# An earlier start of the output projection, an eleventh chunk place and gates that travel with the row numbers, in a two-layer RWKV-7 / latent-attention encoder with experts

## The chip, the cores and the metric

The kernel runs on one core of a Trainium2 chip. The metric is the device time in microseconds (us) of one execution, as the median of several runs; lower is better. Engines are named as in the profile: PE (TensorE), PEld (its weight loads), DVE (VectorE), ACT (ScalarE), POOL (GpSimd), SP (SyncE, which here only issues DMAs).

## The reference

One sequence of 512 tokens, width 1024, two layers. Layer 0 mixes tokens by a bidirectional RWKV-7 recurrence (16 heads of 64), layer 1 by multi-head latent attention. Behind either mixer stands an expert-choice mixture of experts: each of 16 experts takes the 64 tokens that score highest for it.

```python
for i in range(DEPTH):                        # DEPTH = 2
    h = rms_norm(x, norm_mix_g[i])
    if i % 2 == 0:
        mix = rwkv7_time_mix(h, ...)          # ends in (y * g) @ w_o
    else:
        mix = mla_mix(h, ...)
    x = x + mix
    x = x + expert_choice_ffn(rms_norm(x, norm_ffn_g[i]), ...)

def expert_choice_ffn(h, w_router, w_gate, w_up, w_down):
    aff = softmax((h @ w_router).astype(float32), axis=-1)
    gates, idx = top_k(swapaxes(aff, 1, 2), 64)          # per expert
    xe = h[b_idx, idx]
    hid = silu(xe @ w_gate) * (xe @ w_up)                # 1024 x 1024 each
    ye = (hid @ w_down) * gates[..., None]
    return zeros_like(h).at[b_idx, idx].add(ye)
```

The expert weights are 2 layers x 16 experts x 3 matrices of 4 MB, all float32; each is read once.

## The kernel before

**The recurrence (layer 0)** runs over eight pairs of heads (`pairs_pe`, `pairs_act`, `pairs_dve`, `pairs_pool`, u = 0 to 7). In each pair PE first multiplies keys and queries (`across`, L833), then inverts small triangular blocks in five levels (`inverse_step`, L875: X, then T and U, with DVE and ACT copies between), then forms state matrices (L1005 to L1057) and runs a chain of seven state steps (L1088, L1070, L1077). While it waits it computes projections of the next pair, one matmul of 128x512 at a time (`proj_piece`, L547). The last pair has no next one: there nothing stands in those gaps. The end of a pair (centre, square, variance, root on POOL, scale, transpose, times gate) is `last_y_...` for the last pair; `ydone_ready` counts finished pairs.

**The output projection** (`out_pe`, L1388) takes eight tiles `out(t, z)`: four blocks of 128 tokens by two halves of 512 columns, each a sum over eight k, one for each pair of heads, so 64 matmuls of 128x512. For layer 0 all of it stands behind the last pair; only what needs the last pair's result waits for it. DVE adds each tile to x (`added`, L1520), and then each block of tokens is squared (ACT), given its root and multiplied by the norm's gain (POOL, L1495 to L1508), transposed (L1398) and multiplied with the router (L1407). `route_dve` makes the softmax, the eight rounds of top-8 (L1574, L1576), the slot numbers, and with `picks` the matrices `pick` (tokens by 2 x 64 slots, ones and zeros) and `pick_gate` (the same times the gates).

**The experts** run over eight pairs of experts (`moe_pe`, i = 0 to 7). A pair uses twelve chunks of weights of 2 MB; `load_chunk` puts chunk g into place g mod 10 (`RING` = 10), and SP issues it when chunk g - 10 has been read by PE (`chunk_read`); chunk 10, the first refill, comes in two halves, the first when half of chunk 0 is used, and chunk 95 in four. The first ten are loaded while PE still projects and routes: chunks 0 to 3 and 8 after `ydone_ready`, then three blocks of normed tokens are stored to memory (`store_tokens`), then 4, 5, 6 and, after the router, 7 and 9. For the first pair of experts PE gathers the tokens by 32 matmuls with `pick` (`gather_first_pe`, L1648), for the others POOL gathers rows from memory by an indirect DMA (L1759) with row numbers that PE and DVE make (`rows_pe` L1637, `rows` L1765). ACT makes tanh into one buffer `th`, DVE makes the two products (L1772, L1777) into `hid`, PE transposes it (L1702), multiplies with the down weights, and adds the experts' rows to the tokens by `combT`, the transposed `pick_gate` (L1658, L1729).

## Time and profile before

| | us |
|---|---|
| median of 3 runs | 2003.29 |
| lowest and highest run | 2002.77, 2010.22 |
| the profiled execution, device time | 2009.6 |
| its span, first to last instruction | 2007.7 |
| mean granted TensorE clock | 0.975 |

The span is what the views below cut up; the profiled execution is 1.9 us longer than its span and 6.3 us longer than the median. In a timeline row the columns are start, duration, engine, line, operation, written<-read and the number of merged instructions; in brackets the idle time of that engine ahead of it and what ended it. A float32 matmul is recorded as two (x16 is eight matmuls of the program). Spans are in us from the first instruction. The last pair of heads lies at 605 to 664 us, the output projection and the routing of layer 0 behind it to 751, its experts to about 1212; routing and experts of layer 1 take 1464 to the end.

### The profile page before, as it was taken

The page shows a single profiled execution, that of the slowest core. Times are in us where ns is not written, and L with a number is a line of the kernel's source. Part 1 is how long each engine was busy: PE and PEld are TensorE (multiplying, and loading weights), DVE is VectorE, ACT ScalarE, POOL GpSimd, SP SyncE. Part 2 cuts the span into 40 slices and gives each one's busy share as a digit, 9 for nine tenths or more (in the row PEclk, how much of TensorE's full clock was granted, in tenths as well). Part 3 has the DMA queues.
Part 4 walks back from the last instruction along what each step waited for, and adds up shares of the span by engine and source line. Part 5 has one row for each costly group of instructions (what it writes and reads, how often), then busy time and mean ns, then how long its engine had stood idle before and what let it go on. Part 6 is the DMA issues. An engine that isn't in the chain of part 4 may idle for free.

```text
span 2007.7 us, 44887 instructions
## 1 busy us (share of the span) xinstructions
PE 1825.1 (91%) x19992; PEld 955.6 (48%) x19992; DVE 798.5 (40%) x1448; ACT 519.6 (26%) x1025; POOL 239.9 (12%) x294
## 2 busy tenths in 40 slices
PE   7899999999997959999988889899995999999987
PEld 4466666666656534333333325566643333333332
DVE  6755755655654241222121113677714211122111
ACT  2344344344443110101101102465511111010100
POOL 2203113213213110000000001112110000000000
PEclk9999999999999979999999999899997999999999
DMA  4101011011003758999999990300064999999997
GB/s 124 35 27 35 24 32 36 24 32 36 24 10 119 273 210 343 426 429 426 428 427 427 427 405 33 117 23 23 12 274 188 410 426 428 427 427 428 426 427 315
DMA packets 85002, 459.98 MB, mean 229 GB/s; under 512 B 16710, under 2 KB 49867, under 8 KB 60235
## 3 DMA queue, kind: packets, MB, share of 16 engines
q1 hardware_dynamic: 82794, 449.78, 54.9%
q0 software_dynamic: 2016, 7.34, 0.9%
q8 instruction: 159, 2.61, 0.5%
q14 instruction: 33, 0.26, 0.0%
HBM read 449.23 MB, written 7.86 MB: 228 GB/s over the span
## 4 chain that ended last, share of the span: by engine, by line
PE 61%; DMA 21%; issue 7%; DVE 5%; ACT 2%; DVEq 1%; POOL 1%; POOLq 1%; SPq 0%; ACTq 0%; PEldq 0%; another core or an unknown queue 0%
DMA arena<-in_moe_w_down 18%; PE banks L1683 17%; PE banks L547 9%; PE banks L875 5%; PE banks L1388 5%; PE banks L1729 5%; DMA arena<-in_moe_w_up 2%; PE banks L2190 2%; PE banks L2055 2%; PE banks L833 1%; PE banks L2215 1%; PE banks L2203 1%; PE banks L1648 1%; PE banks L564 1%; PE banks L824 1%
## 5 line engine op out<-in xcount | busy, mean ns | idle before, releaser
L1683 PE MATMUL banks<-arena 128*64 128x512 f32 x3072 | 684.2, 598 | 53.1 <-DMA arena<-in_moe_w_down 35.9
L1683 PEld LDWEIGHTS banks<-arena 128*64 128x64 f32 x3072 | 222.3, 137 | 478.5 <-issue 434.3
L1788 DVE TENSOR_TENSOR arena<-arena,banks 128x512 f32<-128x512 f32 x128 | 88.0, 688 | 330.2 <-PE banks L1729 330.2
L547 PE MATMUL banks<-arena 128*128 128x512 f32 x384 | 187.2, 613 | 2.6 <-ACT arena L587 2.6
L875 PE MATMUL banks<-arena 64*64 64x64 f32 x7168 | 148.0, 225 | 32.3 <-issue 27.0
L875 PEld LDWEIGHTS banks<-arena 64*64 64x64 f32 x7168 | 135.6, 139 | 76.5 <-issue 62.7
L1227 POOL TENSOR_TENSOR arena<-arena 128x512 f32<-128x512 f32 x80 | 102.6, 1309 | 436.4 <-DVE arena L1284 436.4
L1742 ACT ACTIVATE arena<-banks 128x512 f32<-128x512 f32 x32 | 19.1, 597 | 411.1 <-PE banks L1683 411.1
L1729 PE MATMUL banks<-arena 128*128 128x512 f32 x256 | 113.7, 597 | 3.0 <-ACTq L1751 3.0
L1777 DVE SCALAR_TENSOR_TENSOR arena<-arena,banks 128x512 f32<-128x512 f32 x32 | 33.7, 1052 | 206.6 <-PE banks L1683 206.6
L1309 DVE TENSOR_TENSOR arena<-banks,arena 128x512 f32<-128x512 f32 x80 | 52.5, 687 | 142.7 <-PE banks L875 142.2
L1388 PE MATMUL banks<-arena 128*128 128x512 f32 x242 | 106.6, 595 | 1.8 <-POOLq L400 1.3
L1759 POOL DMA_INDIRECT arena<-out_dram,small x14 | 13.6, 969 | 779.8 <-DVE small L1765 718.7
L547 PEld LDWEIGHTS banks<-arena 128*128 128x128 f32 x384 | 66.6, 189 | 68.6 <-issue 62.0
L1772 DVE SCALAR_TENSOR_TENSOR arena<-arena,banks 128x512 f32<-128x512 f32 x32 | 22.0, 688 | 186.9 <-ACT arena L1742 186.9
L1750 ACT COPY arena<-banks 64x512 f32<-64x512 f32 x64 | 37.1, 580 | 179.0 <-PE banks L1683 178.6
L1729 PEld LDWEIGHTS banks<-arena 128*128 128x128 f32 x256 | 47.3, 190 | 59.4 <-issue 58.2
L1745 ACT COPY arena<-banks 128x512 f32<-128x512 f32 x32 | 18.8, 586 | 206.1 <-PE banks L1702 206.1
L1388 PEld LDWEIGHTS banks<-arena 128*128 128x128 f32 x242 | 44.9, 190 | 55.3 <-issue 55.3
L1165 ACT COPY arena<-banks 128x512 f32<-128x512 f32 x64 | 38.2, 597 | 108.6 <-PE banks L875 108.6
L2055 PE MATMUL banks<-arena 128*128 128x192 f32 (+1 forms) x320 | 61.7, 347 | 1.1 <-DVE arena L1958 1.1
L2190 PE MATMUL banks<-arena 96*128 96x512 f32 x128 | 60.5, 618 | 1.6 <-POOLq L400 1.6
(301 smaller groups left out, 2205.2 us busy)
## 6 DMA issues: line engine op xcount, KB each, us to landing
arena<-in_moe_w_gate SPq DMA_DIRECT2D x64, 2048.0 KB, 36.3
arena<-in_moe_w_up SPq DMA_DIRECT2D x64, 2048.0 KB, 38.2
arena<-in_moe_w_down SPq DMA_DIRECT2D x60, 2048.0 KB, 39.0
out_dram<-arena SPq DMA_DIRECT2D x12, 512.0 KB, 2.7
arena<-in_x SPq DMA_DIRECT2D x8, 512.0 KB, 6.0
arena<-in_rw_wr SPq DMA_DIRECT2D x8, 512.0 KB, 4.9
arena<-in_rw_wk SPq DMA_DIRECT2D x8, 512.0 KB, 3.6
arena<-in_rw_wv SPq DMA_DIRECT2D x8, 512.0 KB, 3.9
```

The source lines that it names most:

```text
L547: last = nc.tensor.matmul(b[:, :], w_sl[:, n, k, :], xmix[n][:, k, :], start=(k == 0), stop=(k == ND - 1))
L875: last = nc.tensor.matmul(v[half[p ^ lands(h, m)], bank, token(n)], st(q, h, m), mv(q, h, m), start=True, stop=True)
L1165: nc.scalar.copy(Tm[:, :, d, :], two_banks(("T", lv, d, u))).then_inc(free[rj[("T", lv, d, u)][0]], 1)
L1227: nc.gpsimd.tensor_tensor(blocks[lv][d].rearrange("p h m j -> p (h m) j"), LRB[d].rearrange("p h m a j -> p (h m) a j")[:, :, 0, :], bc(le ...
L1309: nc.vector.tensor_tensor(Xm[d].rearrange("p (h m) j -> p h m j", h=2), two_banks(name).rearrange("p h (m j) -> p h m j", j=CH), bc(eye.un ...
L1388: last = nc.tensor.matmul(b[:, :], yT[n][:, k, tile(t)], wo_at[n][:, k, z * 512:(z + 1) * 512], start=(k == 0), stop=(k == ND - 1), skip_g ...
L1683: last = nc.tensor.matmul(b[z * CAP:(z + 1) * CAP, :], st[:, k, :], ring[g % RING][:, k, z * 512:(z + 1) * 512], start=(c % 2 == 0 and k = ...
L1729: nc.tensor.matmul(b[:, :], combT[:, t * P:(t + 1) * P], ye[:, z * 512:(z + 1) * 512], start=True, stop=True).then_inc(full[COMB[j]], 1)
L1750: nc.scalar.copy(ye[e * CAP:(e + 1) * CAP, z * 512:(z + 1) * 512], b[z * CAP:(z + 1) * CAP, :])
L1788: nc.vector.tensor_tensor(xs, xs, b[:, :], ALU.add).then_inc(free[COMB[j]], 1)
L2055: last = nc.tensor.matmul(b[:, y * width:(y + 1) * width], cT[:, n0 + j, t * P:(t + 1) * P], w[:, j, :], start=(j == 0), stop=(j == n - 1))
L2190: nc.tensor.matmul(b[:, :], qkT[h][0][0:QK, t * P:(t + 1) * P], qkT[h][1][0:QK, :], start=True, stop=True).then_inc(full[aj[("S", u, h, t) ...
```

## The change

Four things in one edit.

- The DMA scratch is set to 4096 (`dynamic_dma_scratch_size`), the arena grows from 51 to 54 x 1024 floats, `th` and `pick_gate` are gone, and an eleventh chunk place stands in the room: `RING` = 11. Chunk 10 is loaded with the first six.
- Layer 0's output projection starts within the last pair of heads: `part_pe` computes k = 0 to 5 of four of the eight tiles (24 matmuls) between the steps of that pair, three of them are added to x there by DVE (`part_added`), and the fourth (`HELD`) stays in its bank. The weights w_o are loaded one pair earlier, x for three blocks of tokens in the last pair. Behind the pair the order of tiles, squares, transposes and roots is another.
- The gates come through the same small matmul as the row numbers (three columns in place of one, `row_cols`); DVE halves them into `half_gate`, and the second product is multiplied by that in place of 0.5. tanh goes directly into `hid`, and both products work in place there. `combT` is the transposed `pick`.
- In the first pair of experts the gather is in two halves, with the first chunk's matmuls between them.

```diff
-RING = 10
+RING = 11
-        ARENA = 51 * 1024
+        ARENA = 54 * 1024
...
+        EARLY = NPAIR - 2
+        def part_pe(pe, t, z, k):
+            if (t, z, k) == (0, 0, 0):
+                pe.wait_ge(ld_wo[0], 16)
+                pe.wait_ge(ld_y, 16)
+                pe.wait_ge(ydone_ready, EARLY)
+            if k == EARLY:
+                pe.wait_ge(ydone_ready, EARLY + 1)
+            b = open_job(pe, rj, ("part", t, z)) if k == 0 else ps[rj[("part", t, z)][0]]
+            last = nc.tensor.matmul(b[:, :], yT[0][:, k, tile(t)], wo_at[0][:, k, z * 512:(z + 1) * 512], start=(k == 0),
+                                    stop=(k == EARLY - 1 and (t, z) != HELD), skip_group_check=((t, z) == HELD))
...
+                def part_added(t, z):
+                    b = job_full(dve, rj, ("part", t, z))
+                    xs = x_sb[:, t, z * 512:(z + 1) * 512]
+                    nc.vector.tensor_tensor(xs, xs, b[:, :], ALU.add).then_inc(free[rj[("part", t, z)][0]], 1)
                 for lv in range(LEVELS):
+                    if lv == 1 and not more:
+                        dve.wait_ge(ld_x2, 16 * 3)
+                        part_added(0, 0)
...
-                out(0, 0, range(ND - 1))
+                out(2, 0, range(ND - 1))
                 last_y_pe(pe)
-                out(0, 1, range(ND - 1))
+                part_pe(pe, *HELD, EARLY)
+                out(2, 1, range(ND - 1))
+                for t, z in ((0, 0), (0, 1), (1, 1)):
+                    out(t, z, range(EARLY, ND - 1))
                 pe.wait_ge(ydone_ready, NPAIR)
+                for t, z in ((0, 0), (0, 1), (1, 0), (1, 1)):
+                    out(t, z, range(ND - 1, ND))
...
 +            def inverse_root(t):
...
+            for t in range(NT):
+                if layer == 1 or t < NT - 1:
+                    inverse_root(t)
+                if layer == 0 and t == NT - 2:
+                    inverse_root(NT - 1)
...
-            nc.vector.tensor_tensor(by_expert(pick_gate), by_expert(pick), of(aff), ALU.mult).then_inc(gate_picked, 1)
...
                     for h in range(2):
+                        if i == 0 and c == 0:
+                            if h:
+                                gather_half_pe(pe, 1, xj)
+                            else:
+                                rows_pe(pe, 0, layer)
+                                combination_pe(pe, 0, xj)
+                            job_read(pe, xj, ("x", 0, h))
                         chunk_into(name, c + h, xeT[:, 4 * h:4 * h + 4, e * CAP:(e + 1) * CAP])
...
-            for g in (0, 1, 2, 3, KEPT + 1) if layer == 0 else (0, 1, 2, 3, 4, KEPT + 1):
+            for g in (0, 1, 2, 3, KEPT + 1, KEPT + 3) if layer == 0 else (0, 1, 2, 3, 4, KEPT + 1, KEPT + 3):
...
-    nc = bacc.Bacc("TRN2", target_bir_lowering=False, num_devices=1)
+    nc = bacc.Bacc("TRN2", target_bir_lowering=False, num_devices=1, dynamic_dma_scratch_size=4096)
```

Three places show what stands in a row on an engine. The first is PE in the last pair of heads, from the first level of the inversion (L875, after the change L874) to the first state matrices; before the change:

```order
L875 MATMUL banks<-arena 64x64 x224
L897 MATMUL banks<-arena 64x64 x32
L875 MATMUL banks<-arena 64x64 x64
L824 MATMUL banks<-ident,arena 128x128 x4
L875 MATMUL banks<-arena 64x64 x160
L1005 MATMUL banks<-arena 64x128 x32
```

The same place after the change, down to the third level; L911 is `part_pe`:

```order
L874 MATMUL banks<-arena 64x64 x32
L911 MATMUL banks<-arena 128x512 x2
L874 MATMUL banks<-arena 64x64 x64
L911 MATMUL banks<-arena 128x512 x4
L874 MATMUL banks<-arena 64x64 x32
L911 MATMUL banks<-arena 128x512 x3
L874 MATMUL banks<-arena 64x64 x64
L911 MATMUL banks<-arena 128x512 x3
L874 MATMUL banks<-arena 64x64 x32
L896 MATMUL banks<-arena 64x64 x32
```

Twelve wide matmuls have come between the steps of the first two levels; six more follow up to L1042 and six between there and the pair's end.

The second place is PE at the beginning of layer 1's experts (layer 0's reads the same), from the second routing transpose on; before the change:

```order
L1450 MATMUL banks<-ident,arena 128x16 x4
L1648 MATMUL banks<-arena 128x128 x32
L1658 MATMUL banks<-ident,arena 128x128 x4
L1683 MATMUL banks<-arena 64x512 x48
L1702 MATMUL banks<-ident,arena 128x128 x4
```

After it:

```order
L1524 MATMUL banks<-ident,arena 128x16 x4
L1757 MATMUL banks<-arena 128x128 x16
L1744 MATMUL banks<-small,arena 128x3 x4
L1764 MATMUL banks<-ident,arena 128x128 x4
L1789 MATMUL banks<-arena 64x512 x8
L1757 MATMUL banks<-arena 128x128 x16
L1789 MATMUL banks<-arena 64x512 x40
```

Chunk 0 (the first x8 of L1789) now stands behind half of the gather, and chunk 1 behind the other half.

The third place is SP ahead of layer 0's experts; before the change, from the store of pair 5's result on:

```order
L2412 DMA out_dram<-arena 128x512 [waits y_done]
L1368 DMA arena<-in_rw_g 128x128 [waits bank_full6]
L1369 DMA arena<-in_rw_g 32x128
L2420 DMA arena<-in_rw_wo 128x8x1024 [waits bank_full7]
L2422 DMA arena<-out_dram 128x6x512 [waits y_stored]
L1540 DMA arena<-in_x 128x1024 [waits ld_low_rank,ld_projection_v,ld_gate,ld_projection_k,bank_full1,ld_projection_r,bank_full6]
L1540 DMA arena<-in_x 128x1024 x3
```

After it:

```order
L2524 DMA arena<-in_rw_wo 128x8x1024 [waits bank_full6]
L2533 DMA out_dram<-arena 128x512 [waits y_done]
L1421 DMA arena<-in_rw_g 128x128 [waits bank_full6]
L1422 DMA arena<-in_rw_g 32x128
L2542 DMA arena<-out_dram 128x6x512 [waits y_stored,bank_full7]
L1648 DMA arena<-in_x 128x1024 x3
L1648 DMA arena<-in_x 128x1024 [waits ld_low_rank,ld_projection_v,ld_gate,ld_projection_k,bank_full1,ld_projection_r,bank_full6]
```

The output weights have moved ahead of the wait for pair 5, and three of the four blocks of x ahead of the last pair's end.

## Rows read from the trace of the kernel before

**Rows 1.** A stretch: us, busy per engine (instructions), PEclk, DMA share, GB/s
```profile
800.00:900.00 100.00, 100.00 (x452) 37.39 (x450) 22.29 (x32) 10.04 (x18) 1.88 (x2) 1.00 1.01 427
```
**Rows 2.** Waits of PE, 780 to 1200: us in total, times, longest
```profile
PE banks L1683 <- DMA arena<-in_moe_w_down: 18.1, 16, 2.6
PE banks L1683 <- DMA arena<-in_moe_w_up: 7.5, 8, 1.1
PE banks L1683 <- DMA arena<-in_moe_w_gate: 1.4, 2, 1.1
```
**Rows 3.** The chain that ended last: eight out-projection matmuls; last tile added; the router's exp
```profile
687.05 6.87 PE banks L1388 x16
...
724.72 0.69 DVE arena L1520
...
730.73 0.27 ACT arena L1481
```
**Rows 4.** Stretches: pair 6 in three parts, then the last pair
```profile
543.30:566.80 23.50, 23.50 (x419) 13.93 (x418) 7.11 (x11) 10.05 (x17) 10.21 (x8) 1.00 0.01 3
566.80:584.00 17.20, 13.74 (x589) 10.65 (x588) 15.71 (x23) 10.33 (x20) 0.00 (x0) 1.00 0.06 20
584.00:605.30 21.30, 20.38 (x537) 13.52 (x540) 12.57 (x29) 6.29 (x16) 0.00 (x0) 1.00 0.03 7
615.70:630.90 15.20, 9.23 (x413) 8.63 (x413) 5.79 (x9) 5.49 (x11) 9.67 (x8) 1.00 0.35 126
630.90:648.20 17.30, 11.99 (x552) 10.83 (x551) 5.16 (x8) 7.17 (x15) 0.00 (x0) 0.90 0.02 4
648.20:664.10 15.90, 14.08 (x492) 11.41 (x492) 5.93 (x17) 4.33 (x12) 0.00 (x0) 1.00 0.02 5
```
**Rows 5.** PE groups by line, 604 to 664: busy, mean ns, idle before and releasers
```profile
L875 PE MATMUL banks<-arena 64*64 64x64 f32 x896 | 19.5, 229 | 10.9 <-issue 9.7 <-DVE arena L1309 1.1
```
**Rows 6.** Timeline: the last pair's end and the turn of its result
```profile
664.26 6.25 PE L1388 MATMUL banks<-arena 128*128 128x512 f32 x14 [0.54 <-ACT arena L1214]
...
670.93 0.65 PE L824 MATMUL banks<-ident,arena 128*128 128x128 f32 x4 [0.42 <-DVE arena L1259]
```
**Rows 7.** Timeline of SP: chunks 4 and 5, then the last block of tokens
```profile
724.71 0.82 SPq L1797 DMA_DIRECT2D arena<-in_moe_w_gate  x2
...
732.05 0.34 SPq L1826 DMA_DIRECT2D out_dram<-arena  x1
```
**Rows 8.** A stretch ahead of them, in the output projection
```profile
710.00:720.00 10.00, 10.00 (x30) 4.92 (x30) 1.41 (x3) 2.89 (x5) 3.22 (x4) 1.00 0.01 5
```
**Rows 9.** Timeline: from the picks of layer 0 to its second refill
```profile
750.00 0.33 SPq L1797 DMA_DIRECT2D arena<-in_moe_w_down  x1
...
750.81 9.74 PE L1648 MATMUL banks<-arena 128*128 128x128 f32 x64 [1.15 <-DVE arena L1597]
...
760.59 0.59 ACT L1737 COPY arena<-banks 128x512 f32<-128x512 f32 x1 [0.31 <-PE banks L1648]
...
761.27 20.82 PE L1683 MATMUL banks<-arena 128*64 128x512 f32 x96 [0.29 <-issue]
763.24 2.04 SPq L1804 DMA_DIRECT2D arena<-in_moe_w_down  x2
768.39 0.33 SPq L1797 DMA_DIRECT2D arena<-in_moe_w_down  x1
```
**Rows 10.** Stretches within the first gather
```profile
750.00:755.00 5.00, 4.19 (x19) 4.19 (x20) 1.39 (x2) 0.00 (x0) 0.00 (x0) 0.50 0.83 296
...
757.00:759.00 2.00, 2.00 (x20) 2.00 (x20) 0.00 (x0) 0.00 (x0) 0.00 (x0) 1.00 0.00 0
```
**Rows 11.** Timeline: the row numbers and the gather for the second pair of experts
```profile
789.63 1.05 PE L1637 MATMUL banks<-small,arena 128*128 128x1 f32 x8
...
792.02 1.23 POOL L1759 DMA_INDIRECT arena<-out_dram,small  x1 [61.40 <-DVE small L1765]
...
805.23 1.09 PE L1668 MATMUL banks<-ident,arena 128*128 128x128 f32 x8
```
**Rows 12.** Line L1759, all 14 gathers
```profile
DMA to landing us min/median/max: 10.7/10.9/12.5
```

More of the change, by code:

```diff
@@ L508, in trunk @@
             more = u < NPAIR - 1
+            order += [] if more else [(("part", 0, 0), 6), (("part", 0, 1), 6)]
             for piece in FILL[:4] if more else []:
@@ L903, in pairs_pe, with parts @@
                 more = u < NPAIR - 1
+                def parts(t, z, *ks):
+                    for k in ks if not more else ():
+                        part_pe(pe, t, z, k)
                 if u:
@@ L1494, in out_pool, with inverse_root @@
             pool.wait_ge(ld_gain[2 * layer + 1], 16)
-            for t in range(NT):
+            def inverse_root(t):
                 pool.wait_ge(sq_ready, t + 1)
@@ L1764, in rows @@
                 b = job_full(dve, xj, ("rows", i))
-                nc.vector.tensor_copy(row_index, b[:, 0:1]).then_inc(free[2], 1)
+                if i:
+                    nc.vector.tensor_copy(row_index, b[:, 0:1])
+                for e in range(2):
+                    for q in half:
+                        nc.vector.tensor_scalar(half_gate[q, e:e + 1], b[half[e], 1 + e:2 + e], 0.5, None, ALU.mult)
+                dve.drain().then_inc(free[2], 1)
+            rows(0)
             for i in range(PAIRS):
```

191 lines of the change are left out of this document (130 added, 61 removed).

## The prediction

> **What bounds the kernel now.** I read the busy time in equal stretches first, to see which engine is full in which phase, then the waits of PE, then the chain of waits between the recurrence and the experts, and last the timeline around the places that are edited. In the experts' phases PE and the DMA engines are both full for the first two pairs or so [rows 1]: 427 GB/s, so a chunk of 2.097 MB takes 2.097/0.427 = 4.91 us. Over 780 to 1200 us PE waited for chunks 18.1 + 7.5 + 1.4 = 27 us [rows 2]. So over a layer PE would be ready 27 us sooner than the weights: once the refills run, a layer of experts ends when its last chunk has landed, and only the instant at which the unbroken stream of refills begins, and how many chunks are in it, count. Ahead of layer 0's experts the bound is another: the chain runs through the output projection on PE, matmul behind matmul (sixteen records, eight matmuls, in 6.87 us: 0.86 us each [rows 3]), then through routing to the picks. While that runs the DMA engines stand still for long [rows 8]. In the last pair of heads nobody is full: PE is busy 9.23 of 15.2 us in the first two levels, 11.99 of 17.3 in the other three, 14.08 of 15.9 in the rest [rows 4], and of its idle time ahead of the inversion's matmuls 9.7 of 10.9 us is "issue", that is, no other engine is named [rows 5].
>
> **Part 1, the output projection moves forward.** 24 of its 64 matmuls leave the stretch behind the last pair: 24 x 0.86 = 20.6 us less [rows 3]. Seven matmuls stay as cover while DVE, ACT and POOL finish the last pair's result: they take 6.25 us and the turn comes at 670.93 [rows 6], as before. The other order costs a little: the first transpose needs bank 4, which tile (1, 1) frees only when DVE has added it behind three others at 0.69 us each [rows 3], some 0.7 us of waiting on PE, with the second tiles' last matmuls queued behind. Net 19.9 us earlier. Behind the last tile (724.72 before [rows 3]) add, square, root, logits and routing stand as before, so all of it reaches the picks.
>
> What the same 24 matmuls cost where they go: at least their busy time less the idle time there. First two levels: twelve matmuls, 10.3 us at 0.86, against 6.0 idle: at least +4.3. Last three levels: six, 5.2 us, against 5.3 idle: at least 0. State part: six, 5.2 against 1.8: at least +3.4. Floor +7.7. From the other side pair 6 shows what such gaps cost when filled with 24 projections and three other wide matmuls: its three parts take 62.0 us, the last pair's 48.4 [rows 4]: +13.6, with DVE work that the last pair hasn't got (35.39 us busy against 16.88). A gap doesn't always stand where a matmul does, so 15 is the ceiling. I take +10.5, between floor and pair 6: +4.5, +1, +5. The three adds on DVE (2.1 us) lie beside a DVE that is busy 11 of 32.5 us there. The w_o load (4 MB) goes into pair 6, where the engines move 3 to 20 GB/s [rows 4], and leaves 3 MB of y and x for the start of the last pair; both are there before the first part needs them, since 3.1 MB at 427 GB/s are 7.4 us from 604.8 and the inversion begins at 615.7.
>
> **Part 2, the DMA chain ahead of layer 0's experts.** The third store of tokens now waits for a scaling that ACT does behind the router's exp, and SP has chunks 4, 5, 6 queued behind it. Counted from the old times and with everything 19.9 - 10.5 = 9.4 us earlier, exp is at 721.3, that store at about 723, and four chunks and two blocks of tokens (1.2 us each) then end at 745. Before, those chunks were issued from 724.71 [rows 7]. The first refill is wanted at 750.8 - 9.4 + 9.9 = 751.3 (below). So 6 us are left and the wait costs nothing; if the store slid by more than that, each us is lost. The eleventh chunk goes into DMA time that is idle [rows 8]: free. POOL's roots and multiplications end some 15 us before the picks: free.
>
> **Part 3, refills, in either layer.** Before, from the picks (PE's gather, 750.81): chunk 0 begins at +10.5, the first refill is issued at +12.4, the second at +17.6, and 85 whole chunks are still to come, that one included [rows 9]. After: half of the gather is 32 records. 19 ran while the granted clock was 0.50, that is 1.2 GHz, by about +4.2 to +4.9; then ten in each us at 2.4 GHz [rows 10]: 6.2 us. Row numbers 1.05 (now ahead of the first pair too) and the turn of the picks 0.55, half of an eight-record turn [rows 11]: chunk 0 begins at +7.8, the first refill is issued at +9.8, chunk 0 ends at +11.3. The other half of the gather 3.2, ACT's copy 0.59 [rows 9] with its hand-overs 0.8, chunk 1 3.5: the second refill is issued at +18.8, 1.2 us later than before, and behind it come 84 chunks in place of 85. So the early first refill gives nothing, since the second can't follow it; the layer's end moves by -4.91 + 1.2 = -3.7 us. Bounds: -7.5 if the stream counts from the first refill (2.6 us earlier), -1.5 if the clock stays at 1.2 GHz through chunk 0. Two layers: -7.4. The Trainium skill ("DMA: Bandwidth & Descriptors", section on the anatomy of one DMA) gives one DMA as 2.0 us plus its bytes over 436 GB/s, which for a chunk is an estimate of 6.8 us; if refills paid the fixed part one after the other, this term would be -5.6 a layer and the sum 3.8 us lower. The 427 GB/s of [rows 1], with every refill its own DMA, speak for transfers that cover each other's fixed part.
>
> **Part 4, gates, tanh, scratch.** One product of 0.69 us on DVE for each pair goes, two tiny multiplications for each expert and a drain come ahead of `free[2]`: the indirect gather is issued perhaps 1 us later than its 792.02. It lands 10.9 us behind its issue [rows 12], at 802.9, and PE asks at 805.23 [rows 11]: 1 us is covered, and a later one still by the 27 us [rows 2]. In-place products with strided rows cost DVE up to 0.4 us more each; DVE is 22% busy [rows 1]: nothing. The smaller scratch: nothing seen for it or against it in the trace; I take 0.
>
> **Sum.** -19.9 + 10.5 - 7.4 = -16.8 us. Against the profiled execution (2009.6, span 2007.7) that is 1992.8; against the median of 2003.29, which I forecast, 1986.5.
>
> **Rivals.**
> - *The gaps swallow the fills.* If the issue stalls go on beside wide matmuls, the last pair grows by the floor of 7.7 and the refills give up to 7.5 each: -19.9 + 7.7 - 12 = -24, 1979. For it: 9.7 us of issue [rows 5]. Against: the first two levels can't take twelve. 0.15.
> - *The fills aren't hidden.* If each pushes the chain it stands in, the last pair grows by 15 to 20: -5 - 7.4 = -12 down to -7, 1991 to 1996. For it: the state part is full on PE already. 0.13.
> - *The eleventh place gives nothing,* because the wait for the second refill or the late stores eat it: -9.4, 1994. 0.10.
> - *Slower: the gather for the next pair of experts.* It is the one thing that uses the scratch, and it now waits for more DVE work. It may land 2.3 us later before PE feels it, and PE may lose 27/7 = 3.9 us at each of seven hand-overs in a layer before it becomes the bound; from 6.2 us on every further us costs 14. If a smaller scratch doubled the 10.9 us: (10.9 - 6.2) x 14 = 66 us, less 16.8: 2052. Against it: one gather in 60 us, all landing within 10.7 to 12.5. The Trainium skill (same page, section on queues and rings) has each DMA engine alternate between the queues that have work, so that a deeper SP queue wouldn't delay POOL's gather; the narrow 10.7 to 12.5 of [rows 12] agrees. 0.06.
> - *It doesn't do what it says:* a part waits for w_o, y or a bank, and the pair stalls by as much as is won: -7.4 or less, 1996 to 2003. 0.06.
>
> **How the numbers follow.** My forecast has 0.50, with its own range of 1978 to 1993: growth of the last pair 7.7 to 15, refills -1.5 to -7.5 a layer. All rivals but the slower one lie in 1978 to 2000; I give 1977 to 1998. About 0.5%, 10 us, is what a measurement of this kernel can tell from no change, so faster means below 1993.3: my forecast, the first rival and a part of the second and third, 0.71; the same: the rest of these and the last, 0.23; slower 0.06.
>
> **What would show it.** In the changed profile: the last pair from the first inversion matmul to the y copies at 59 us in place of 48.4, PE's issue waits there nearly gone; from its end to the picks about 20 us less; the first refill about 10 us and the second about 19 us behind the first gather matmul; PE's waits for chunks in a layer down from 27 to 22 or so; gathers still landing in 11 us. I am wrong if the last pair grows by over 15, if SP's chunks 4 to 7 land behind the picks, or if PE waits for the gathered rows.

## The result, and the profile after

| | before | after |
|---|---|---|
| median (4 runs each) | 2005.18 us | 1991.09 us |
| lowest and highest | 2002.77, 2010.22 | 1989.47, 1992.05 |
| profiled execution; its span | 2009.6; 2007.7 | 1990.3; 1988.6 |

The ratio is 0.9923, with a 95% interval of 0.9908 to 0.9938. That is 15.4 us of 2005.18 (12 to 18), where I had forecast 16.8; the median of 1991.09 lies 4.6 us above the 1986.5 I named and within the range. Of these 4.6 us 1.9 come from the kernel before: its median was 2003.29 when I forecast and is 2005.18 with a fourth run. The profiled execution of before lay 4.4 us above its median and that of after 0.8 us below, so the two spans differ by 19.1 us, more than the medians do.

I cut both spans at the same places: the first inversion matmul of the last pair, the turn of its last result, the first gather matmul behind the picks of each layer, and the first `combT` matmul of each layer's last expert pair.

| stretch | before | after | difference | forecast |
|---|---|---|---|---|
| start to the last pair's inversion | 615.7 | 616.2 | +0.5 | 0 |
| inversion to the turn of the last result | 55.2 | 63.7 | +8.4 | +10.5 |
| turn to the picks (with the w_o matmuls) | 79.9 | 60.3 | -19.6 | -19.9 |
| experts of layer 0 | 454.6 | 449.2 | -5.4 | -3.7 |
| attention and routing of layer 1 | 337.5 | 338.4 | +0.9 | 0 |
| experts of layer 1 | 453.9 | 449.9 | -4.0 | -3.7 |

Stretches of the changed kernel (us, busy per engine with instructions, PEclk, DMA share, GB/s), pair 6 in three parts, then the last pair in three, as in [rows 4]:

```profile
539.90:563.50 23.60, 23.60 (x423) 14.02 (x426) 7.11 (x11) 10.05 (x17) 10.22 (x8) 1.00 0.01 3
563.50:584.50 21.00, 16.67 (x604) 12.54 (x608) 17.75 (x26) 10.40 (x20) 0.00 (x0) 0.84 0.58 216
584.50:605.10 20.60, 19.68 (x530) 12.96 (x524) 10.71 (x26) 6.29 (x15) 0.00 (x0) 1.00 0.03 7
616.20:635.50 19.30, 19.30 (x413) 12.17 (x412) 5.48 (x9) 5.48 (x11) 9.22 (x8) 1.00 0.01 3
635.50:652.90 17.40, 16.39 (x597) 11.44 (x596) 5.91 (x9) 7.06 (x15) 0.00 (x0) 1.00 0.02 4
652.90:672.60 19.70, 19.23 (x506) 12.59 (x505) 6.71 (x18) 3.75 (x10) 0.00 (x0) 1.00 0.01 3
```

The last pair is full on PE now: 54.9 of 56.4 us, where [rows 4] have 35.3 of 48.4. Its first two levels grew from 15.2 to 19.3 us, the other three from 17.3 to 17.4, the state part (to the first of the seven cover matmuls) from 16.0 to 19.7. The groups of PE at 604 to 672 us (busy, mean ns, idle before and releasers) show that the issue waits of [rows 5] have gone from the inversion:

```profile
L911 PE MATMUL banks<-arena 128*128 128x512 f32 x48 | 24.5, 623 | 0.0
L874 PE MATMUL banks<-arena 64*64 64x64 f32 x896 | 17.8, 220 | 0.5 <-ACT arena L1206 0.4
L832 PE MATMUL banks<-arena 64*64 64x128 f32 x128 | 4.6, 271 | 2.1 <-issue 2.1
```

The new thing stands in pair 6. Its middle part, where w_o is now loaded at 216 GB/s, has the clock at 0.84 and takes longer. The timeline of PE there, after the change:

```profile
563.41 1.16 PE L874 MATMUL banks<-arena 64*64 64x64 f32 x64
...
568.69 0.34 PE L874 MATMUL banks<-arena 64*64 64x64 f32 x8
572.04 1.77 PE L874 MATMUL banks<-arena 64*64 64x64 f32 x56 [3.01 <-issue]
573.75 2.08 PE L563 MATMUL banks<-arena 64*128 64x512 f32 x4
```

And the same matmuls before the change:

```profile
566.81 1.16 PE L875 MATMUL banks<-arena 64*64 64x64 f32 x64
...
572.09 1.38 PE L875 MATMUL banks<-arena 64*64 64x64 f32 x64
573.40 1.13 PE L564 MATMUL banks<-arena 64*128 64x512 f32 x4
```

Within one group of 64 records that ran in 1.38 us before, PE now stops for 3.01 us on nothing that the profile names, and the four wide records behind the stop take 2.08 us in place of 1.13. The same stretch of 524 records, cut at the same two matmuls, in three kernels (after; before; one with the load in eight slices, below):

```profile
563.41:581.92 18.51, 14.18 (x524) 10.87 (x523) 15.32 (x22) 9.33 (x18) 0.00 (x0) 0.82 0.65 244
```
```profile
566.81:581.84 15.03, 11.57 (x524) 9.29 (x523) 13.69 (x20) 9.23 (x18) 0.00 (x0) 1.00 0.01 4
```
```profile
562.35:577.38 15.03, 11.59 (x524) 9.29 (x523) 13.69 (x20) 9.23 (x18) 0.00 (x0) 1.00 0.34 108
```

The table hides those 3.5 us, because this execution happened to reach pair 6 3.4 us sooner than the profiled one of before (529.5 against 532.9 us). The code up to there gives no reason for it, and the kernel before with the smaller scratch alone (below) reached it 3.7 us sooner than the kernel before, too.

In the experts, the timeline after the change, from the last of the first eleven chunks to the second refill (compare [rows 9]):

```profile
739.36 0.33 SPq L1915 DMA_DIRECT2D arena<-in_moe_w_down  x1
...
740.17 5.87 PE L1757 MATMUL banks<-arena 128*128 128x128 f32 x32 [1.15 <-DVE arena L1706]
...
745.87 0.95 PE L1744 MATMUL banks<-small,arena 128*128 128x3 f32 x8
...
747.61 0.66 PE L1764 MATMUL banks<-ident,arena 128*128 128x128 f32 x4 [0.78 <-DVEq L1884]
...
748.20 3.65 PE L1789 MATMUL banks<-arena 128*64 128x512 f32 x16
...
750.18 2.04 SPq L1922 DMA_DIRECT2D arena<-in_moe_w_down  x2
751.78 3.84 PE L1757 MATMUL banks<-arena 128*128 128x128 f32 x32
...
759.99 0.33 SPq L1915 DMA_DIRECT2D arena<-in_moe_w_gate  x1
```

Chunk 0 begins at +8.0 (forecast +7.8), the first refill is issued at +10.0 (+9.8), the second at +19.8 (+18.8). PE waits for chunks, 770 to 1190 us (us in total, times, longest):

```profile
PE banks L1789 <- DMA arena<-in_moe_w_down: 14.8, 12, 3.2
PE banks L1789 <- DMA arena<-in_moe_w_up: 4.2, 5, 1.2
```

19.0 us in place of the 27 of [rows 2]. The gathers of the other pairs land 0.5 us later in the median than those of [rows 12] and within the same bounds:

```profile
DMA to landing us min/median/max: 10.8/11.4/12.2
```

### The profile page after: what moved, and what is told of

It reads as the page before. It is cut to its first block and busy times, and to the rows that moved or that the text cites. A ratio compares the mean times of both kernels' runs of the same rounds, so it can differ in the third digit from the quotient of the medians.

```text
span 1988.6 us, 44942 instructions
## 1 busy us (share of the span) xinstructions
PE 1823.3 (92%) x20008; PEld 948.1 (48%) x20008; DVE 812.0 (41%) x1501; ACT 532.7 (27%) x1025; POOL 240.3 (12%) x294
## 5 line engine op out<-in xcount | busy, mean ns | idle before, releaser
L1789 PE MATMUL banks<-arena 128*64 128x512 f32 x3072 | 683.5, 598 | 40.9 <-DMA arena<-in_moe_w_down 28.8
L1789 PEld LDWEIGHTS banks<-arena 128*64 128x64 f32 x3072 | 218.7, 137 | 467.3 <-issue 431.7
L546 PE MATMUL banks<-arena 128*128 128x512 f32 x384 | 187.8, 615 | 2.3 <-ACT arena L586 2.0
L874 PE MATMUL banks<-arena 64*64 64x64 f32 x7168 | 147.3, 225 | 25.7 <-issue 22.5
L874 PEld LDWEIGHTS banks<-arena 64*64 64x64 f32 x7168 | 134.5, 138 | 74.9 <-issue 64.0
L1856 ACT ACTIVATE arena<-banks 128x512 f32<-128x512 f32 x32 | 34.1, 1067 | 395.4 <-PE banks L1789 395.4
L1893 DVE SCALAR_TENSOR_TENSOR arena<-arena,banks 128x512 f32<-128x512 f32 x32 | 34.0, 1064 | 219.4 <-ACT arena L1856 219.4
L1843 PE MATMUL banks<-arena 128*128 128x512 f32 x256 | 113.7, 597 | 3.0 <-ACTq L1865 3.0
L1896 DVE SCALAR_TENSOR_TENSOR arena<-arena,small,banks 128x512 f32<-128x512 f32 x32 | 35.5, 1109 | 173.9 <-PE banks L1789 173.9
L546 PEld LDWEIGHTS banks<-arena 128*128 128x128 f32 x384 | 66.7, 190 | 67.6 <-issue 61.0
L1449 PE MATMUL banks<-arena 128*128 128x512 f32 x192 | 84.6, 594 | 1.3 <-POOLq L398 1.3
L1843 PEld LDWEIGHTS banks<-arena 128*128 128x128 f32 x256 | 47.3, 190 | 59.5 <-issue 58.3
L2348 ACT ACTIVATE arena<-banks,small 128x512 f32<-128x512 f32 x64 | 49.8, 778 | 42.9 <-DVE small L2384 23.3
```

Of the source, the lines that this page charges most:

```text
L546: last = nc.tensor.matmul(b[:, :], w_sl[:, n, k, :], xmix[n][:, k, :], start=(k == 0), stop=(k == ND - 1))
L874: last = nc.tensor.matmul(v[half[p ^ lands(h, m)], bank, token(n)], st(q, h, m), mv(q, h, m), start=True, stop=True)
L1449: last = nc.tensor.matmul(b[:, :], yT[n][:, k, tile(t)], wo_at[n][:, k, z * 512:(z + 1) * 512], start=(k == first and (n, t, z) != (1, 0, ...
L1789: last = nc.tensor.matmul(b[z * CAP:(z + 1) * CAP, :], st[:, k, :], ring[g % RING][:, k, z * 512:(z + 1) * 512], start=(c % 2 == 0 and k = ...
L1843: nc.tensor.matmul(b[:, :], combT[:, t * P:(t + 1) * P], ye[:, z * 512:(z + 1) * 512], start=True, stop=True).then_inc(full[COMB[j]], 1)
L2348: nc.scalar.activation(prob[h][:, t, :], b[:, :], ACT.Exp, bias=nmx[:, n:n + 1], scale=q_scale[u % 2][:, 2 * t + h:2 * t + h + 1], accum_o ...
```

## The experiments

Twelve kernels; ratios are to the kernel before, run on the same chip in the same session. Theory A is the prediction's; the letters of the rivals are those of the expectations.

### The eleventh place taken away

```diff
-RING = 11
+RING = 10
-            for g in (0, 1, 2, 3, KEPT + 1, KEPT + 3) if layer == 0 else (0, 1, 2, 3, 4, KEPT + 1, KEPT + 3):
+            for g in (0, 1, 2, 3, KEPT + 1) if layer == 0 else (0, 1, 2, 3, 4, KEPT + 1):
```

> The changed kernel with ten chunk places in place of eleven, all else as changed. Theory A (a layer of experts ends when an unbroken stream of refills ends, and the stream counts from the second refill): one more chunk of 4.9 us in either layer, 9.8 us slower than the changed kernel, about 2001 us, ratio to before 0.998; PE's waits for chunks in a layer go back from 19 us to 24 or more. Theory B (the eleventh place is worth nothing, the gain of layer 0's and layer 1's experts, 5.4 and 4.0 us in the two profiles, comes from the split gather and its early first refill): 1991 to 1993 us, ratio 0.993.

Measured: 1999.75 us, ratio 0.9978 (0.9967 to 0.9989). The experts take 454.1 and 454.5 us, as before the change (454.6, 453.9), against 449.2 and 449.9 with eleven places: 5.0 and 4.6 us for one chunk more, the 4.91 us that 2.097 MB take at 427 GB/s. PE waits 24.7 us for chunks in layer 0, as the expectation's "24 or more" has it. Theory A holds in its count of chunks. With ten places, everything else that the change does in the experts is worth -0.5 and +0.6 us.

### The early projection taken away

The order of before on PE, DVE and SP is restored around the last pair (`part_pe` and `part_added` gone, w_o loaded at the beginning of the last pair); experts as changed.

```diff
-                    if lv == 0:
-                        parts(0, 0, 0, 1)
...
-                out(2, 0, range(ND - 1))
+                out(0, 0, range(ND - 1))
```

> The changed kernel with the output projection of layer 0, its order behind the last pair, and the loads of w_o and x as they were before the change; eleven places, gates and split gather stay. Theory A: the last pair takes 48.4 us again from the first inversion matmul to the y copies (56.4 in the changed kernel) and the picks come 10.6 us later: 1991.1 + 10.6 = 2001.7, ratio 0.998. Theory C (DMA ahead of the experts is the bound in the changed kernel, so an earlier pick is partly lost): only 4 to 8 us slower, 1995 to 1999, and the first refill relative to the picks earlier than in the changed kernel.

Measured: 1996.18 us, 0.9961 (0.9949 to 0.9974): by the ratios 7.6 us above the changed kernel, not 10.6. Inversion to turn 54.7 us, turn to picks 79.9 us: both as before. So Part 1 is worth 19.6 - 9.0 = 10.6 us in the stretches that the prediction cut, but some 3 us of it are lost elsewhere. The time is the one that theory C gave (1995 to 1999), and its sign is there too, but small: the first refill is issued at +9.5 behind the picks here and at +10.0 in the changed kernel, and layer 0's experts take 0.6 us less. The rest of the loss stands in pair 6 and behind it: up to the last pair's first inversion matmul 83.0 us here, 86.7 in the changed kernel (counted as in the table on w_o below).

### The gather whole again, and the row numbers late

In the first of these both halves are gathered by the loop of before, ahead of row numbers, turn and chunk 0. In the second the halves come one behind the other, and row numbers and turn stand behind chunk 1:

```diff
             gather_half_pe(pe, 0, xj)
+            gather_half_pe(pe, 1, xj)
...
+                        if i == 0 and c == 0 and h == 1:
+                            rows_pe(pe, 0, layer)
+                            combination_pe(pe, 0, xj)
```

> The changed kernel with the first pair's gather in one piece ahead of chunk 0, as before; row numbers, gates and the turn of the picks still ahead of chunk 0. Theory A: chunk 0 begins later (about +12 us behind the picks' first gather matmul in place of +8.0) and so does the first refill, but the second refill is issued at +19, in place of +19.8 and +20.2, so the time is the same within 1.5 us, 1990 to 1992. Theory B (the early first refill is what counts): 3 us later in either layer, 1997 us, ratio 0.995.

> The changed kernel with the whole gather first (the first half's matmuls complete, then the second's), then chunks 0 and 1, and only then the small matmul for the row numbers and gates and the turn of the picks. Theory A: second refill issued at +17 behind the first gather matmul, 3 us earlier than in the changed kernel, in either layer: 1985 to 1987 us, ratio 0.990. Theory B (first refill counts; it is issued at +12 in place of +10): 1993 us or more.

| | first, second refill | experts, layer 0 and 1 | ratio |
|---|---|---|---|
| changed kernel | +10.0, +19.8 | 449.2, 449.9 | 0.9923 (0.9908 to 0.9938) |
| whole gather | +13.5, +18.6 | 450.4, 451.1 | 0.9932 (0.9915 to 0.9949) |
| whole, rows late | +12.2, +17.4 | 448.0, 450.5 | 0.9932 (0.9916 to 0.9948) |

Medians 1991.01 and 1990.76 us. The prediction's rule that the stream counts from the second refill asked for a gain of 1.2 us a layer with the whole gather, and there was a loss of 1.2 in both; with the rows late it asked for 2.4 and more, and there was a gain of 1.2 and a loss of 0.5. The rule fell, although the first time lies in the range that theory A gave; the second lies between theory A (1985 to 1987) and theory B (1993 and more). Nor does the first refill alone decide. From the bytes moved in the 40 us behind the first gather matmul, at 427 GB/s, the DMA engines stood idle for 6.8, 6.7 and 6.2 us in layer 0 and 11.8, 11.5 and 10.6 us in layer 1, in the order of the table: a refill moved forward opens a gap behind it that is nearly as long. These idle times don't rank the kernels either, since the whole gather has 0.1 to 0.3 us less of them and takes 1.2 us more. What decides about the last microsecond is open. In the six kernels in which I took it (before, after and the first four here), the first `combT` matmul of the last pair comes 4.1 to 4.2 us behind the last packet of the last chunk, so the layer ends with the stream.

### The gates alone, and the scratch alone

The kernel before with the three-column matmul, `half_gate` and in-place products; and the kernel before with the smaller scratch:

```diff
-                last = nc.tensor.matmul(b[:, 0:1], pick[:, t, :], token_f[:, t:t + 1], start=(t == 0), stop=(t == NT - 1))
+                last = nc.tensor.matmul(b[:, 0:3], pick[:, t, :], row_cols[:, t, i, :], start=(t == 0), stop=(t == NT - 1))
```
```diff
-    nc = bacc.Bacc("TRN2", target_bir_lowering=False, num_devices=1)
+    nc = bacc.Bacc("TRN2", target_bir_lowering=False, num_devices=1, dynamic_dma_scratch_size=4096)
```

> The kernel before with the gates' part of the change alone: gates and row number of each token picked in one three-column matmul per expert pair, the products with tanh in place, the gather of the rows still issued in one piece and ten chunk places. The prediction put the gates, the tanh in its own rows and the wait on the stores at 0, since they hide behind the chunks. Theory A: ratio 1.000 within 0.002, 2002 to 2007. Theory F (the in-place products or the later row numbers reach the stream): slower by 0.4 us and more for each of 64 products, 2010 and above.

> The kernel before with the smaller DMA scratch alone, and nothing else. Theory A (the scratch is only room): ratio 1.000 within 0.001. Theory G (a smaller ring of descriptors holds up the gathers that GpSimd issues): each of 64 gathers lands later by what its issue waits; the first matmuls of each expert wait for it, a ratio of 1.005 and more, 2014 and above.

Measured: gates 2008.93 us, 1.0016 (1.0006 to 1.0026), slower by 3.2 us (1.2 to 5.2), more than theory A's 2007 and less than theory F's 2010; scratch 2006.44 us, 1.0000 (0.9991 to 1.0009), its gathers landing in 10.7/10.9/12.2 us. The scratch is only room (a layer has 7 gathers, 14 in all, not the 64 of the expectation). The gates are not free by themselves: their row numbers are needed ahead of the first chunk, and PE waits for DVE's columns. The timeline of the gates alone, layer 0 (start, us, engine, line, then the idle time in brackets):

```profile
750.60 9.24 PE L1645 MATMUL banks<-arena 128*128 128x128 f32 x64 [1.15 <-DVE arena L1596]
...
759.68 0.95 PE L1634 MATMUL banks<-small,arena 128*128 128x3 f32 x8
...
761.42 0.66 PE L1663 MATMUL banks<-ident,arena 128*128 128x128 f32 x4 [0.79 <-DVEq L1775]
```

Chunk 0 begins at +11.4 (layer 1: +12.3) in place of +10.5 (+10.8 in the kernel with the scratch alone), the refills follow as late, and the experts take 455.5 and 455.8 us, 1 to 2 us more than before. In the changed kernel the halved gather hides this: chunk 0 needs half the gather only. tanh takes 1067 ns (597 before) and the first product 1064 (688), both written with a stride, as the prediction allowed for; no wait of PE on either of them shows.

### Six of the early matmuls moved behind the pair

```diff
-                parts(1, 0, 0)
...
-                part_pe(pe, *HELD, EARLY)
+                for k in range(EARLY + 1):
+                    part_pe(pe, *HELD, k)
```

> The changed kernel, with six of the 24 matmuls of the early w_o projection, those that it spreads through the state part of the last pair, moved behind the pair again. Prediction's theory A: the state part of the last pair falls from 19.7 us to 16.0 to 16.7 us, the stretch from the last result turned to the gather grows by 6 matmuls of 0.86 us, 60.3 to 65.5 us: net 1 to 2 us slower, 1992 to 1993.5. Theory H (the state part grew by late fetches and bank waits, not by the matmuls written into it): it stays at 19 us or more, and the time is 1995 to 1997.

Measured: 1990.01 us, 0.9921 (0.9907 to 0.9934). In the profile the state part takes 15.7 us (19.7) and turn to picks 65.5 us (60.3): the six cost 4.0 us within the pair and 5.2 us behind it, so their early place is worth 1.1 us in these stretches, as theory A has it, and theory H is out. The time doesn't show it: theory A gave 1992 to 1993.5, and the ratio is that of the changed kernel.

### w_o in four slices, in one piece later, and in eight slices

```diff
+            part_of = lambda n: slice(n * ND // 4, (n + 1) * ND // 4)
+            wo_slice = lambda n: sp.dma_start(wo_at[0][:, part_of(n), :], wo[0][:, part_of(n), :]).then_inc(ld_wo[0], 16)
...
-                    sp.dma_start(wo_at[0], wo[0]).then_inc(ld_wo[0], 16)
+                    wo_slice(0)
...
+                    wo_slice(1)
+                    job_full(sp, rj, ("PQ", 1, 1, u))
+                    wo_slice(2)
```

> The changed kernel, with the 4 MB of w_o loaded in four slices of 1 MB spread over the pair before the last, at the end of its r projection, behind its store of y, behind the last of its PQ jobs and behind its g job, instead of in one piece at the end of the r projection. Why: in the traces so far the pair before the last takes 72.3 us in the kernel before and 72.6 us where w_o is loaded in the last pair, but 75.5, 76.9, 75.5 and 76.9 us in the four kernels that load it in one piece here, with one or two stops of TensorE of 3.0 us on nothing that the profile names, while two fetches of instructions on queue 8 that stand 3.3 to 4.3 us apart elsewhere stand 6.6 and 6.0 us apart inside the load. Theory D (a fetch of instructions is held up behind the packets of one long load): a slice of 1 MB holds a fetch up by at most about 2.4 us, TensorE's stops shrink, the pair takes 72.5 to 73.5 us, and the time is 1987 to 1989 (ratio to the kernel before about 0.9915 times, 2 to 4 us under the changed kernel's). Theory E (it is the bytes, by their traffic in the memory or the on-chip memory, and not the length of the one load): the pair stays at 75 to 77 us, the time at 1990 to 1992.

> The changed kernel, with w_o loaded in one piece, but issued some 15 us later in the pair before the last, behind the store of y (at about 579 us instead of 563.5 us), so that its packets run beside the projection's long matmuls mixed with the state part, not beside the inversion's short ones. Theory D (a fetch held up by a long load): it stops TensorE here too where it runs through its instructions quickly; 25 to 28 matmuls a microsecond against 33 there leave it some more slack, so the pair takes 73.5 to 75.5 us and the time is 1988 to 1991. If only the place mattered and not the length: 72.5 us and 1987 to 1988.

> The changed kernel, with w_o loaded in eight slices of 0.5 MB, 2.5 to 6 us apart, between the end of the r projection and the g job of the pair before the last. Four slices had TensorE's two stops on nothing at 1.3 and 1.1 us instead of one of 3.0 (or 2.2 and 3.1), the clock at full through the pair, and the pair at 74.2 us; one piece issued 15 us later had stops of 2.1 and 2.0 us, the clock down to 0.71 for a while, and the pair at 78.8 us. Theory D (a fetch of instructions stands behind the packets of a load): a slice of 0.5 MB holds it up by at most 1.2 us, no stop over 1 us is left, the pair takes 72.3 to 73.3 us and the time is 1987 to 1989. Theory E (the bytes): 74 us and more as with four slices, 1990 to 1991.

The last of them once more with the late gather order, and once with its last two slices earlier:

> The eight slices, and in the first expert pair of each layer both halves gathered in a row ahead of chunk 0, with the row numbers and the combination matrix behind chunk 1 (the form with the first two refills at 12.2 and 17.3 us behind the gather's first matmul). Apart the second edit gave 1990.8 us where the changed kernel has 1991.1. Theory D for the slices as with the eight slices alone, and nothing from the second edit: 1987 to 1989. If the earlier second refill is worth something after all: 1985 to 1987.

> The eight slices again (1984.7 us, the best so far), with the last two issued some 12 us earlier, behind two of the state part's jobs at about 587 and 590 us instead of at 601 and 602 us, where they ran into the load of y and x that begins the last pair. Theory D (a fetch of instructions stands behind the packets of a load, and slices 3 us and more apart hold none up by more than 1.2 us): the stretch from the start of the pair before the last to the first inversion matmul of the last pair, 82.8 us in the kernel before, 86.7 in the changed kernel and 83.5 with the eight slices, is 82.8 to 83.8 us, no stop of TensorE on nothing is over 1.5 us there, and the time is 1984 to 1987. If the 1984.7 us was chance, and slices are worth only what four of them gave: 85 us there, and 1988 to 1990.

| w_o | kernel | pair 6, us | up to the last pair's inversion, us | time | ratio |
|---|---|---|---|---|---|
| in the last pair | before | 72.3 | 82.8 | 2005.18 | 1 |
| in the last pair | no early projection | 72.6 | 83.0 | 1996.18 | 0.9961 |
| one piece at 563 us | changed kernel | 75.5 | 86.7 | 1991.09 | 0.9923 |
| one piece at 563 us | whole gather | 75.5 | 87.9 | 1991.01 | 0.9932 |
| one piece at 563 us | whole, rows late | 76.9 | 89.4 | 1990.76 | 0.9932 |
| one piece at 563 us | six behind | 75.4 | 88.0 | 1990.01 | 0.9921 |
| one piece at 563 us | ten places | 76.9 | 89.4 | 1999.75 | 0.9978 |
| one piece at 578 us | later | 78.8 | 89.8 | 1994.40 | 0.9945 (0.9931 to 0.9959) |
| four slices | | 74.2 | 85.2 | 1990.20 | 0.9917 (0.9903 to 0.9931) |
| eight slices | | 74.5 | 83.5 | 1984.65 | 0.9892 (0.9877 to 0.9907) |
| eight, rows late | | 73.7 | 83.0 | 1988.98 | 0.9916 (0.9901 to 0.9931) |
| eight, last two earlier | | 74.5 | 87.0 | 1988.71 | 0.9916 (0.9902 to 0.9929) |

The fourth column counts from one and the same point, 0.7 us behind pair 6's first matmul, to the last pair's first inversion matmul.

The four slices and the later piece did worse than theory D had said (72.5 to 73.5 us and 73.5 to 75.5 us for pair 6, 1987 to 1989 and 1988 to 1991 for the time), and the place of the later piece is worse, not better. The later piece has its stops elsewhere, in the state part, behind its load, which is issued at 578.0 us (timeline of PE):

```profile
580.48 1.96 PE L1042 MATMUL banks<-arena 64*64 64x128 f32 x58
584.56 0.44 PE L1042 MATMUL banks<-arena 64*64 64x128 f32 x6 [2.13 <-issue]
...
587.10 1.70 PE L1076 MATMUL banks<-arena 64*64 64x128 f32 x53
590.85 0.90 PE L1076 MATMUL banks<-arena 64*64 64x128 f32 x10 [2.04 <-issue]
```

With eight slices the first stop has shrunk to 0.27 us, which the kernel with w_o in the last pair has at this record too:

```profile
567.63 0.34 PE L874 MATMUL banks<-arena 64*64 64x64 f32 x8
568.24 1.04 PE L874 MATMUL banks<-arena 64*64 64x64 f32 x56 [0.27 <-issue]
```

Up to 577.38 us this kernel is level with the one before; in the rest of pair 6 it loses 2.2 us (a stop of 1.3 us at L1042 among it), which is why pair 6 took 74.5 us and not the 73.3 at most that theory D gave it. The four slices have the same stop of 1.3 us at L1042 and took 74.2 us: within pair 6 eight slices are no better than four.

They need no load. The 9.7 us of "issue" in [rows 5] are seven such stops, the last three of them while the DMA engines moved 4 GB/s [rows 4]. Timeline of PE in the last pair, before the change:

```profile
618.10 3.42 PE L875 MATMUL banks<-arena 64*64 64x64 f32 x127 [1.26 <-issue]
623.16 1.73 PE L875 MATMUL banks<-arena 64*64 64x64 f32 x97 [1.63 <-issue]
625.27 0.68 PE L875 MATMUL banks<-arena 64*64 64x64 f32 x29 [0.38 <-DVE arena L1309]
626.90 2.27 PE L875 MATMUL banks<-arena 64*64 64x64 f32 x127 [0.95 <-issue]
630.97 0.82 PE L875 MATMUL banks<-arena 64*64 64x64 f32 x36 [1.80 <-issue]
```

From one stop to the next there are 127, 126 and 127 matmul records, each with a weight load: some 256 instructions. PE runs through them in 2.3 to 3.4 us, and the fetches there begin 3.9 to 5.0 us apart. That is why the early w_o matmuls fitted in so cheaply: a wide one keeps PE busy for longer than a short one, for as many instructions. In the changed kernel a single such stop of 0.5 us is left between the first inversion matmul and the turn; in the kernel without the early projection, all else changed, eight of 0.7 to 1.9 us are back.

What makes a fetch late beside a load is less clear. Theory D, a fetch that stands behind the packets of one long load, is right in that whole loads do it, but the length of the single load isn't all of it: behind 577 us the store of y and two slices of 0.5 MB follow each other without a pause for 5.6 us, the fetches stand 6.9 us apart there (5.1 before the change), and that is the stop at L1042. In the kernel with four slices, one slice of 1 MB (3.6 us of packets) left 5.2 us between two fetches, another (4.1 us) 3.8. Theory E, the bytes themselves, isn't out either: it gave pair 6 74 us and more, as measured, and of the eight slices only three fell into the stretch that came back to 15.03 us (108 GB/s in place of 244), of the four slices one, with 15.03 us as well. What the traces of pair 6 show is that fetches were late where the packets of loads and stores ran on for over 5 us, and not where 2 us of them stood alone.

The Trainium skill ("Runtime: NRT & Kernel Launch", section on instruction fetch mechanics) says that an engine fetches its instructions in blocks of 16 KiB, 256 instructions, through a DMA queue of its own, at a cost "mostly hidden". The size agrees with the trace, and so do the 127 records; hidden the fetch is neither beside this load nor in the last pair of before. The stop of 3.0 us also costs the clock: within it the granted clock fell to 0.50, that is 1.2 GHz, and it stayed there until 577 us, which the four and the eight slices avoid in pair 6. Stretches of the changed kernel from within the stop on, and one of the eight slices:

```profile
570.00:571.00 1.00, 0.00 (x0) 0.00 (x0) 0.93 (x2) 0.00 (x0) 0.00 (x0) 0.69 1.02 406
571.00:572.00 1.00, 0.00 (x0) 0.00 (x0) 0.85 (x2) 0.00 (x0) 0.00 (x0) 0.50 1.00 414
...
576.00:577.00 1.00, 1.00 (x48) 1.00 (x47) 1.00 (x3) 0.05 (x1) 0.00 (x0) 0.50 0.06 25
```
```profile
568.00:572.00 4.00, 2.33 (x73) 1.46 (x76) 3.70 (x7) 0.52 (x1) 0.00 (x0) 1.00 0.41 130
```

What the slices are worth in all is less sharp. Against four kernels with the one piece at 563 us (the one with ten places left out; mean ratio 0.9927), the four kernels with slices (mean 0.9910) are 3.4 us faster, by some 2 us either way, as far as these means go; without the best of the four it would be 2.2. Of the eight slices, 1984.65 us is the best time of all and its interval just doesn't overlap with the changed kernel's. But its near twin with the last slices earlier gave 1988.71, with 87.0 us up to the inversion where 82.8 to 83.8 were expected and a stop of 2.0 where none over 1.5 was: that is the time for the case that the 1984.65 was chance. The eight slices with the late gather order gave 1988.98, which is theory D's time with nothing from the order. The profiles of the eight slices and of that twin differ at the beginning of the last pair, where y and x are loaded (3 MB): one has a stop of 0.7 us there and takes 9.0 us to the first inversion, the other stops for 2.0 us and takes 12.5. Which one a kernel gets may depend on where its next fetch falls against that load; this isn't shown, and I didn't find what sets it. The kernel before has such a stop there too, of 1.5 us. Slicing x and y as well was not tried.

## Why the prediction was right, and where it wasn't

- **What bounds the kernel.** Right, but for one thing that the prediction left without a name, the 9.7 us of "issue" in the last pair: they were waits for instruction fetches, and the fills took their place. For the rest: the experts end with the stream of chunks in the kernels where I took its last packet, and the stretch ahead of them with PE's w_o matmuls.
- **The -19.9 us behind the pair.** Right: -19.6.
- **The +10.5 us within it.** The mechanism was right and the size 2 us too large: +4.1 in the first two levels (forecast +4.5), +0.1 in the last three (+1), +3.7 in the state part (+5), and +0.6 in the chain that makes the last result. Without that 0.6 it is close to the floor of 7.7: PE filled nearly all of its idle time. Moving six matmuls back showed the state part's share, 4.0 us for 5.2 us of work.
- **w_o loaded in pair 6 at no cost.** This step failed. I looked whether the DMA engines and the on-chip room were free there, and they were; I didn't look who else uses the DMA engines. Over pair 6 and on to the last pair's inversion the changed kernel takes 3.9 us more than the one before, and four others with the same load 5 to 7, because the load holds up PE's instructions and with that the clock. That the sum came out so near is in part luck, since other errors hide it: 16.8 forecast, plus 2.1 for the last pair that grew less, plus 2.0 for the experts, less 3.9 for this, 0.9 for layer 1's middle and 0.3 behind the pair, is 15.8, where the ratio says 15.4.
- **6 us of slack for the late store.** Harmless, but the slack was nearly gone: the loads ahead of the refills ran until 750 us, where the first refill was issued at 750.18, not until 745.
- **-3.7 us a layer from the refills.** Measured -5.4 and -4.0, inside the bounds. The chunk's 4.91 us was right: 5.0 and 4.6 in the experiment, and not the 6.8 that the prediction estimated for refills that pay a fixed part in turn (its source there, the Trainium skill, "DMA: Bandwidth & Descriptors", section on the anatomy of one DMA, gives that sum for a DMA issued by GpSimd; SP issues the refills). The +1.2 us for the later second refill was wrong, with the rule behind it: with ten places the first refill came 2.2 us sooner than before and the second 2.4 us later, and the experts took 0.5 us less and 0.6 more. So the early first refill pays for the late second one.
- **Gates, tanh and scratch at nothing.** Right for the scratch. For the gates right only because of the halved gather; alone they cost 3.2 us. I had costed the row numbers ahead of chunk 0 in Part 3, as a shift of 1.05 us, but not DVE's share behind them (0.78 us of waiting).
- **Rivals.** The gaps swallowed the fills almost as far as the first rival had it, and the refills did not; the slower rival needed gathers landing later, and they land at 11.4 us in place of 10.9, less than the 2.3 us later that PE would have felt.

## What to carry to other kernels

A large DMA that is moved into a stretch where "the DMA engines are idle" is not free if an engine there runs through short instructions quickly: look at the spacing of the instruction fetches, cut the load into slices with some microseconds between them, and keep them from running into other loads and stores. A stop on "issue" in a dense run of short instructions, one for each 256 of them, is a wait for the next block, and wide instructions put into the run cost little. When a stream has a start that several small edits compete for, measure to its last packet, and don't judge by the instant of one refill. And compare stretches between the same two instructions, since a difference of 3.5 us hid behind an equal accident in the first 530 us.
